# LayerNorm of the convolution branch moved from the compression and prompt stages into the decode passes, and three more right-half projection steps in decode pass 3

## The chip, the cores and the metric

The kernel runs on one core of a Trainium2 chip. The time is the device time of one execution in microseconds, and the number compared is the median over executions. The engines are called by the profile's names: PE is TensorE (matmuls and transposes), PEld its weight loads, DVE is VectorE, ACT ScalarE, POOL GpSimd, SP SyncE, which in this kernel only issues DMAs.

## What is computed

The program is one inference step of a decoder with two layers, for a prompt of 512 rows and 8 sequences of 8 new rows, 576 rows in all, all in float32. A layer has two branches side by side, attention (compressed, selected and window keys) and a Conformer convolution, then one output projection, then a gated feed-forward. The part of the reference that the change touches:

```python
def layer_norm(x, g, b):
    mu = jnp.mean(xf, -1, keepdims=True)
    var = jnp.mean(jnp.square(xf - mu), -1, keepdims=True)
    y = (xf - mu) * lax.rsqrt(var + EPS) * g + b

def conformer_conv(u, buf, w, b, ln_g, ln_b):
    xx = jnp.concatenate([buf, u], 1)
    y = dwconv_valid(xx, w) + b                      # width 31, 512 channels
    y = jax.nn.silu(layer_norm(y, ln_g, ln_b))

def merge_and_ffn(...):
    c, conv_state = conformer_conv(...)
    x = x + jnp.concatenate([o_nsa, c], -1) @ w_out
```

`c` is needed only by the product with `w_out`, which reads it as the last four of eight blocks of 128 channels.

## The kernel before

Channels lie on partitions. `catT` holds the input of the output projection as 8 tiles of 128 channels by 576 rows: tiles 0 to 3 are attention, tiles 4 to 7 (`catT[:, CT + c]`, CT = 4) the convolution. 576 rows are handled as a left and a right half of 288 (HN); `halves()` views a row of 576 as 2x288.

Every engine has its own written-out program, and the order in it is the order in which it works. They meet at named semaphores: `wait_ge(*count("x"))` waits for the next signal of `x`. On DVE, `step(...)` makes an instruction be waited for by the next one. A layer runs through glu, project, compress, prompt, decode, mix, expand and contract.

- **compress** makes compressed keys and values. `hidden` (one of its products: 16 steps j, of 254 columns) accumulates in a PSUM bank that must have been read by DVE's `gelu_in` of an earlier job, which signals `cmp_in`. `keys_T`, `keys_second`, `cmp_scores` and `prompt_values` are short products behind it, each after a small piece of DVE and ACT work. The LayerNorm of the convolution stands here too: `means` (8 matmuls of a matrix of ones with the 4 convolution tiles) sums over channels, DVE's `ln_centre` subtracts the mean in `catT`, ACT squares (`ln_square`), 8 more matmuls (`square_sum`) sum the squares, and DVE's `ln_var` reads them.
- **prompt** is the prompt attention in 16 steps v. DVE's `mask(v)` reads the scores of `scores(v)`, ACT takes the exponentials, DVE's `weight(v)` scales, PE's `turn(v)` transposes and `weigh(v)` applies the values. ACT takes the root of the variance between steps 0 and 1; DVE's reciprocals (`ln_root`) stand behind `weight(1)` and `weight(4)`, and `ln_scale(c)` behind v = 5, 8, 9, 12.
- **decode** has four passes p, two sequences in each. PE makes scores over 2048 keys, then work that DVE's selection (30x30 comparisons, then masks) hides: in passes 0 to 2 steps of `hidden`, in pass 3 steps of the output projection. It then waits for `s_exped` (ACT's exponential of the masked scores), transposes 23 blocks, and weighs the values. Between the last products stand `keys_T`, which wait for DVE's `key_norm` (`kn_made`), and at the end the transpose of the output, which waits for DVE's `o_ready`. A pass also gates one convolution tile (tanh on ACT, two operations on DVE, `conv_done`).
- **mix** finishes the output projection. A unit n is one tile of 128 output channels, 8 steps k of 288 columns for each half. Left halves of units 0 to 3 and eight convolution steps (k = 4 to 7) of right halves (`right_conv`) are done in pass 3, the others here.

SP works through one list as well: keys of the next pass go out when `slc_made` comes, the weights of `w_out` and `w_up` when units are done. `hist`, the convolution history of the next layer (128x4x304), is loaded into the tail of `XC` while layer 0 compresses.

## Time and profile before

| | us |
|---|---|
| median of 3 runs | 1894.15 |
| lowest and highest | 1892.86, 1899.56 |
| profiled execution | 1898.77 |
| its span | 1897.0 |

The span is what the trace covers, and the profiled execution took 1.8 us more than it. Layer 0 fills about the first half of the span, layer 1 the second. In layer 0 compress ends near 220 us, prompt near 308, the four decode passes begin at 308, 345, 382 and 421, and mix at 452. Layer 1 goes through the same places some 935 to 942 us later.

A reader needs three views: the first part of the page (busy time of each engine), the timeline, which merges equal instructions and shows before each the time that its engine sat idle and what ended it, and the windows, which give the busy time of the engines and the granted TensorE clock (1.00 is full) in chosen stretches. In the timeline a float32 matmul counts as two records, so x16 there is 8 matmuls of the program.

### The profile page before, as it was taken

What the parts mean: (1) busy time and instruction counts of PE and PEld (TensorE: products, weight loads), DVE (VectorE), ACT (ScalarE), POOL (GpSimd) and SP (SyncE); (2) the same over time, 40 slices, a digit from 0 to 9 for tenths busy, and PEclk for the clock granted to TensorE, in tenths of its full rate; (3) what the DMA queues carried; (4) which work ended last, traced back from release to release, by engine and by line L of the source; (5) the groups of instructions that cost most, each with busy time, mean ns of one, the idle gap of its engine ahead of it and who ended that gap; (6) DMA issues with size and microseconds to landing.
All of it is one profiled execution on the core that took longest, in us unless ns stands there. A gap on an engine that the chain in (4) does not pass through costs nothing.

```text
span 1897.0 us, 26865 instructions
## 1 busy us (share of the span) xinstructions
PE 1855.6 (98%) x10198; PEld 1414.7 (75%) x10198; DVE 1253.0 (66%) x2636; ACT 371.6 (20%) x957; POOL 118.4 (6%) x219
## 2 busy tenths in 40 slices
PE   8999999999999999999999999998999999999999
PEld 7767677777777777777777676776777777777777
DVE  5899896453666766673268998944536667676631
ACT  2013474322100000100001125832221000000000
POOL 1011400010000000000000113000000000000000
PEclk9999999999999999999999999999999999999999
DMA  7303563673121212131241044057531121222211
GB/s 282 127 1 89 157 204 127 205 241 109 63 67 67 89 67 89 58 133 62 85 161 59 1 141 121 2 179 233 168 109 56 67 89 67 89 67 87 93 61 50
DMA packets 110851, 200.28 MB, mean 106 GB/s; under 512 B 13793, under 2 KB 81650, under 8 KB 105730
## 3 DMA queue, kind: packets, MB, share of 16 engines
q1 hardware_dynamic: 105154, 168.17, 26.6%
q0 software_dynamic: 5568, 30.39, 4.6%
q8 instruction: 81, 1.33, 0.3%
q14 instruction: 48, 0.39, 0.1%
HBM read 190.82 MB, written 15.94 MB: 109 GB/s over the span
## 4 chain that ended last, share of the span: by engine, by line
PE 71%; DVE 20%; SPq 5%; issue 2%; ACT 1%; DMA 1%; POOL 0%; DVEq 0%
PE ps L1048 30%; PE ps L1113 15%; DVE catT L1598 7%; PE ps L612 7%; PE ps L599 5%; PE ps L748 4%; SPq L363 2%; PE ps L851 2%; PE ps L814 2%; PE ps L833 2%; SPq L345 1%; PE ps L899 1%; DVE catT L1605 1%; PE ps L984 1%; DVE rC L1604 1%
## 5 line engine op out<-in xcount | busy, mean ns | idle before, releaser
L1598 DVE SCALAR_TENSOR_TENSOR catT<-XC,par,catT 128x512 f32<-128x512 f32 x240 | 180.3, 751 | 7.5
L2097 DVE TENSOR_TENSOR xT<-xT,ps 128x288 f32<-128x288 f32 (+3 forms) x55 | 41.7, 758 | 153.2 <-PE ps L1113 152.9
L1048 PE MATMUL ps<-catT,rD 128*128 128x288 f32 x528 | 131.6, 406 | 0.0
L1048 PEld LDWEIGHTS ps<-catT,rD 128*128 128x128 f32 x528 | 100.3, 190 | 27.7
L1048 PE MATMUL ps<-catT,XC 128*128 128x288 f32 x480 | 119.8, 406 | 0.4 <-DVE rD L2011 0.4
L748 PE MATMUL ps<-WR,rD 128*128 128x254 f32 (+1 forms) x512 | 119.2, 382 | 0.2
L1463 ACT ACTIVATE rD<-rD 128x592 f32<-128x592 f32 x44 | 30.7, 697 | 450.2 <-DVE rD L2039 450.2
L1048 PE MATMUL ps<-rA,WR 128*128 128x288 f32 x448 | 117.8, 406 | 0.0
L1048 PEld LDWEIGHTS ps<-catT,XC 128*128 128x128 f32 x480 | 91.0, 190 | 26.2 <-issue 1.2
L748 PEld LDWEIGHTS ps<-WR,rD 128*128 128x128 f32 x512 | 93.3, 187 | 18.7 <-issue 2.9
L1048 PEld LDWEIGHTS ps<-rA,WR 128*128 128x128 f32 x448 | 85.1, 190 | 23.5
L612 PE MATMUL ps<-catT,WR 128*128 128x288 f32 x384 | 98.8, 410 | 1.9 <-ACT catT L1212 1.1
L599 PE MATMUL ps<-rA,WR 128*128 128x288 f32 x384 | 93.4, 406 | 0.0
L1048 PE MATMUL ps<-rA,rB 128*128 128x288 f32 x336 | 88.6, 407 | 2.8 <-DVEq L2034 2.8
L748 PE MATMUL ps<-rD 128*128 128x254 f32 x384 | 88.8, 379 | 0.0
L599 PEld LDWEIGHTS ps<-rA,WR 128*128 128x128 f32 x384 | 73.0, 190 | 20.2
L612 PEld LDWEIGHTS ps<-catT,WR 128*128 128x128 f32 x384 | 71.2, 190 | 21.8 <-issue 2.0
L1212 ACT ACTIVATE rC<-ps 128x326 f32<-128x326 f32 (+8 forms) x136 | 48.6, 393 | 191.7 <-PE ps L647 118.9
L1048 PEld LDWEIGHTS ps<-rA,rB 128*128 128x128 f32 x336 | 63.7, 190 | 21.1 <-DVEq L2034 3.7
L748 PEld LDWEIGHTS ps<-rD 128*128 128x128 f32 x384 | 69.7, 188 | 10.3 <-issue 0.7
L647 PE MATMUL ps<-rB,rA 128*128 128x326 f32 x256 | 71.6, 437 | 0.0
L2003 DVE TENSOR_TENSOR rD<-rD,ps 128x288 f32<-128x288 f32 x42 | 19.1, 454 | 77.7 <-PE ps L1048 77.7
(371 smaller groups left out, 3341.8 us busy)
## 6 DMA issues: line engine op xcount, KB each, us to landing
WR<-in_w_up SPq DMA_DIRECT2D x56, 512.0 KB, 3.8
WR<-in_kvc SPq DMA_DIRECT2D x128, 128.0 KB, 2.4
rB<-in_ksT SPq DMA_DIRECT2D x256, 64.0 KB
rB<-in_w_up SPq DMA_DIRECT2D x32, 512.0 KB, 4.4
rD<-in_kvc SPq DMA_DIRECT2D x96, 128.0 KB
rD<-in_w_down SPq DMA_DIRECT2D x8, 1408.0 KB, 7.7
rB<-in_w_down SPq DMA_DIRECT2D x6, 1408.0 KB, 6.2
WR<-in_w_glu SPq DMA_DIRECT2D x16, 512.0 KB, 3.7
```

Of the source, the lines that this page charges most:

```text
L363: sp.dma_start(ksT[e][:, P * g:P * (g + 1)], I["ksT"][l, ds(page, 1)].rearrange("a p e -> (a p) e")).then_inc(sh["ks_in"], 16)
L599: ins = mm(ps[:, bank + hf, 0:HN], w[:, k * P:(k + 1) * P], rhs[:, k, hf * HN:(hf + 1) * HN], start=k == 0, stop=k == K - 1)
L612: ins = mm(ps[:, bank, 0:HN], w[:, k, :], rhs[:, k, hf * HN:(hf + 1) * HN], start=k == first, stop=k == last)
L647: ins = mm(ps[0:m, 4 * (t % 2) + ch, 0:CHW], hT[:, k, t * P:t * P + m], weights(ch, k), start=k == 0, stop=k == KD - 1)
L748: ins = mm(out[:, 0:2 * nb].rearrange("p (c h) -> p c h", h=2), w1[n][:, j, :], chunks[:, j // NPAIR:j // NPAIR + nb, o:o + 2], start=j == ...
L814: ins = mm(ps[:, 2 * e + h, 0:n], q[h], KT[hp[h], e, 0:n], start=True, stop=True)
L833: ins = tr(ps[:, bank, j * P:(j + 1) * P], pb[2 * h + e][:, k * P:(k + 1) * P], ident[:, :])
L1048: ins = mm(ps[:, bank, 0:HN], w[:, k, :], h[:, k, :], start=k == 0, stop=k == 3)
L1113: ins = mm(ps[:, bank, 0:HN], w(k), h(k), start=k == 0, stop=k == FH - 1)
L1212: return act.activation(out, in_, ACT.Copy)
L1598: ins = stt(yc[:, 0:SEQ], xc[:, k:k + SEQ], w, yc[:, 0:SEQ], ALU.mult, ALU.add)
L2097: step(tt(x, x, src, ALU.add))
```

## The change

LayerNorm loses its sums over four tiles. DVE first adds the four convolution tiles into one (`ln_add`, behind `weight(4)`), and PE sums that one over channels with 2 matmuls (`conv_sum`) before `weigh(15)`. DVE subtracts the mean (`ln_centre`) behind the last `weight`. In decode pass 0 DVE squares and adds the tiles itself (`ln_squares`, 7 operations), PE runs `conv_sum` a second time ahead of the value products, and DVE reads it behind the first `key_norm` (`ln_var`). ACT takes the root in pass 1, DVE the reciprocal and two `ln_scale` there, two more in pass 2, then three gates (`conv_gate`) behind pass 2's first `key_norm`; the fourth stays in pass 3. On PE the sums leave compress, and 10 of the 16 steps of a `hidden` that stood in prompt take the place of `means`, now in bank 7; the other 6 stay in prompt. In pass 3, `right_conv` covers 11 steps and not 8: three more stand ahead of the wait for `s_exped`; `mix` has 3 fewer. The buffers of LayerNorm move into the tail of `XC`, so the load of `hist` moves behind pass 3. ACT's four `Square` and its root between prompt steps go away.

```diff
@@ SP, layer
                 sp.wait_ge(*count("uc_out", 16))
-                if l + 1 < DEPTH:
-                    sp.dma_start(XC[:, :, XS0:XW], I["hist"][l + 1]...)
...
+                sp.wait_ge(sh["conv_done"], CT * (l + 1))
+                if l + 1 < DEPTH:
+                    sp.dma_start(XC[:, :, XS0:XW], I["hist"][l + 1]...)
                 down(l, 0)
@@ PE, compress
                 keys_second(l, 1, NCP, prompt_pick, CG[0])
-                means(l)
+                hidden(l, 2, 3, 1, js=range(10))
                 keys_T(NCP)
...
                 prompt_values()
-                for c in range(CT):
-                    square_sum(c, 2, lnsq, CT)
                 keys_T(NCS)
+            def conv_sum():
+                pe.wait_ge(*count("u_ready"))
+                for hf in range(2):
+                    ins = mm(ps[:, 1 + 2 * hf, 0:HN], ones[:, :], lnu[:, hf, :], start=True, stop=True)
+                ins.then_inc(sh["u_summed"], 1)
@@ PE, prompt
                 pe.wait_ge(*count("cs_max"))
-                pe.wait_ge(sh["var_made"], 6 * l + 4)
                 scores(0)
+                hidden(l, 2, 3, 1, js=range(10, 13))
+                scores(1)
+                hidden(l, 2, 3, 1, js=range(13, 16))
                 pe.wait_ge(sh["cmp_in"], 16 * l + 5)
-                hidden(l, 2, 3, 1, js=range(8), bank=4)
-                scores(1)
-                hidden(l, 2, 3, 1, js=range(8, 16), bank=4)
...
+                pe.wait_ge(*count("masked"))
+                conv_sum()
                 weigh(15)
@@ PE, decode
+                    if p == 0:
+                        pe.wait_ge(*count("u_read", 2))
...
                         right_conv(0, 4, CT, KD)
+                        pe.wait_ge(sh["x_left"], KD * l + 2)
+                        right_conv(1, 7, CT, KD - 1)
                     pe.wait_ge(*count("s_exped"))
...
                         pe.wait_ge(*count("st_kept", 2))
+                        if p == 0:
+                            conv_sum()
                     else:
-                        right_conv(1, 6, CT, CT + 2)
+                        right_conv(1, 7, KD - 1, KD)
+                        pe.wait_ge(sh["x_left"], KD * l + 4)
+                        right_conv(2, 5, CT, CT + 1)
...
-                        right_conv(1, 6, CT + 2, KD)
+                        right_conv(2, 5, CT + 1, KD - 1)
@@ ACT
-                root(lnrs[0])
-                root(lnrs[1])
...
+                    if p == 1:
+                        root(lnv)
...
+                        if p == 2:
+                            act.wait_ge(*count("ln_made", 4))
+                            for c in range(3):
+                                act.activation((halves(thl), lnu, lnv)[c], halves(catT[:, CT + c, :]), ACT.Tanh, scale=0.5)...
@@ DVE
+            def ln_squares():
+                y = [halves(catT[:, CT + c, :]) for c in range(CT)]
+                tt(lnu, y[0], y[0], ALU.mult)
+                step(tt(lnv, y[1], y[1], ALU.mult))
+                for c in range(2, CT):
+                    step(tt(lnu, lnu, lnv, ALU.add))
+                    step(tt(lnv, y[c], y[c], ALU.mult))
+                tt(lnu, lnu, lnv, ALU.add).then_inc(sh["u_ready"], 1)
+            def conv_gate(c, th):
+                y = halves(catT[:, CT + c, :])
+                dve.wait_ge(*count("ln_tanh"))
+                step(ts(th, th, 0.5, 0.5, ALU.mult, ALU.add))
+                tt(y, y, th, ALU.mult).then_inc(sh["conv_done"], 1)
@@ DVE, prompt
-                    if v in (1, 4):
-                        ln_root(v // 4)
+                    if v == 4:
+                        ln_add(l)
...
-                    if v in (5, 8, 9, 12):
-                        ln_scale((5, 8, 9, 12).index(v))
+                ln_centre()
@@ DVE, decode
                         gelu_out(*halves_of[1])
+                        if p == 0:
+                            ln_squares()
+                        if p == 1:
+                            ln_root()
                         key_means(NCS)
...
                         key_norm(NCS)
+                        if p == 0:
+                            ln_var()
+                        if p == 1:
+                            ln_scale(0)
+                            ln_scale(1)
+                        if p == 2:
+                            for c in range(3):
+                                conv_gate(c, (halves(thl), lnu, lnv)[c])
                         key_means(NCS)
```

Three places of the order show what moves. The first is PE at the end of compress. L691 is `keys_second`, L735 `keys_T`, L722 `cmp_scores`, L713 `prompt_values`, L664 `means`, L577 `square_sum`, L814 `scores`, L748 `hidden`; before:

```order
L691 MATMUL ps<-par,rC 31x64 x2
L664 MATMUL ps<-catT,ones 128x288 x8
L735 MATMUL ps<-ident,KN 128x31
L691 MATMUL ps<-par,rC 127x64 x2
L722 MATMUL ps<-rC 128x64 x16
L691 MATMUL ps<-par,rC 127x64 x2
L713 MATMUL ps<-par,rC 31x64 x8
L577 MATMUL ps<-rA,ones 128x288 x8
L735 MATMUL ps<-ident,KN 128x127
L814 MATMUL ps<-rC 128x256 x4
L748 MATMUL ps<-WR,rD 128x254 x8
```

and after, where the same functions are L682, L726, L713, L704, L809 and L739:

```order
L682 MATMUL ps<-par,rC 31x64 x2
L739 MATMUL ps<-WR,rD 128x254 x10
L726 MATMUL ps<-ident,KN 128x31
L682 MATMUL ps<-par,rC 127x64 x2
L713 MATMUL ps<-rC 128x64 x16
L682 MATMUL ps<-par,rC 127x64 x2
L704 MATMUL ps<-par,rC 31x64 x8
L726 MATMUL ps<-ident,KN 128x127
L809 MATMUL ps<-rC 128x256 x4
L739 MATMUL ps<-WR,rD 128x254 x3
```

Both groups of eight matmuls with `ones` are gone, ten steps of `hidden` stand where the first group stood, and nothing stands where the second did.

The second place is pass 0 of decode, PE between the last small product and the weighing of the values (L984, after: L985). Before:

```order
L691 MATMUL ps<-par,rC 127x64 [waits cmp_g,vct_kept,st_kept]
L691 MATMUL ps<-par,rC 127x64
L984 MATMUL ps<-rC,rB 32x64 [waits vs_in,st_kept]
L984 MATMUL ps<-rC,rB 32x64 x23
L748 MATMUL ps<-WR,rD 128x254 [waits cmp_in]
L984 MATMUL ps<-rC,rB 32x64 x24
```

and after:

```order
L682 MATMUL ps<-par,rC 127x64 [waits cmp_g,vct_kept,st_kept]
L682 MATMUL ps<-par,rC 127x64
L789 MATMUL ps<-XC,ones 128x288 [waits u_ready,st_kept]
L789 MATMUL ps<-XC,ones 128x288
L985 MATMUL ps<-rC,rB 32x64 [waits vs_in]
L985 MATMUL ps<-rC,rB 32x64 x23
```

The two matmuls with `ones` stand ahead of all value products, and they wait for DVE's `u_ready`. What DVE does there, from `gelu_out` (L1721, after: L1745) to `key_means` (L1725, after: L1749), before:

```order
L1716 SCALAR_TENSOR_TENSOR rC<-rC 128x254 [waits dve_step]
L1721 SCALAR_TENSOR_TENSOR rC<-rC 128x254 [waits cmp_th]
L1725 TENSOR_REDUCE KM<-KN 127x2 [waits kn_sq]
L1726 TENSOR_SCALAR KM<-KM 127x2 [waits dve_step]
L1913 TENSOR_SCALAR st<-st 128x2 [waits s_exped]
```

and after:

```order
L1740 SCALAR_TENSOR_TENSOR rC<-rC 128x254 [waits dve_step]
L1745 SCALAR_TENSOR_TENSOR rC<-rC 128x254 [waits cmp_th]
L1708 TENSOR_TENSOR XC<-catT 128x2x288
L1709 TENSOR_TENSOR XC<-catT 128x2x288
L1711 TENSOR_TENSOR XC<-XC 128x2x288 [waits dve_step]
L1712 TENSOR_TENSOR XC<-catT 128x2x288 [waits dve_step]
L1711 TENSOR_TENSOR XC<-XC 128x2x288 [waits dve_step]
L1712 TENSOR_TENSOR XC<-catT 128x2x288 [waits dve_step]
L1713 TENSOR_TENSOR XC<-XC 128x2x288 [waits dve_step]
L1749 TENSOR_REDUCE KM<-KN 127x2 [waits kn_sq]
L1750 TENSOR_SCALAR KM<-KM 127x2 [waits dve_step]
```

Seven operations on 128x576 elements now stand between the two, and `u_ready` comes with the last of them.

The third place is PE in pass 3, around the wait for `s_exped` ahead of the 16 transposes (L885, after: L880). Before:

```order
L612 MATMUL ps<-catT,WR 128x288 x21
L885 MATMUL ps<-ident,rA 128x128 x16
L885 MATMUL ps<-ident,rA 8x128 x2
L885 MATMUL ps<-ident,rA 127x128
L612 MATMUL ps<-catT,WR 128x288 x2
L984 MATMUL ps<-rC,rB 32x64 x48
```

and after:

```order
L611 MATMUL ps<-catT,WR 128x288 x24
L880 MATMUL ps<-ident,rA 128x128 x16
L880 MATMUL ps<-ident,rA 8x128 x2
L880 MATMUL ps<-ident,rA 127x128
L611 MATMUL ps<-catT,WR 128x288 x2
L985 MATMUL ps<-rC,rB 32x64 x48
```

The run of projection steps ahead of the transposes is longer by three, and what stands behind them is as long as before.

## Rows read from the trace of the kernel before

**Rows 1.** The page, its first part: busy time and instructions of each engine
```profile
PE 1855.6 (98%) x10198; PEld 1414.7 (75%) x10198; DVE 1253.0 (66%) x2636; ACT 371.6 (20%) x957; POOL 118.4 (6%) x219
```

**Rows 2.** Timeline: start us, duration us, engine, line, operation, xcount [idle before <-releaser]
```profile
464.34 15.68 PE L599 MATMUL ps<-catT,WR 128*128 128x288 f32 x64
```

**Rows 3.** Timeline of PE, end of the compression of layer 0 and the first turn
```profile
205.29 4.15 PE L664 MATMUL ps<-catT,ones 128*128 128x288 f32 x16
...
209.71 0.24 PE L735 MATMUL ps<-ident,KN 31*128 31x31 f32 x1 [0.27 <-DVE KN L1732]
...
210.95 3.74 PE L722 MATMUL ps<-rC 128*128 128x64 f32 x32
...
215.48 4.39 PE L577 MATMUL ps<-rA,ones 128*128 128x288 f32 x16
...
220.88 1.13 PE L814 MATMUL ps<-rC 64*128 64x256 f32 x8 [0.90 <-DVE rB L1698]
...
233.57 0.66 PE L833 MATMUL ps<-ident,rA 128*128 128x128 f32 x4 [0.65 <-DVE rC L1716]
```

**Rows 4.** Timeline of DVE in the same stretch
```profile
207.40 0.49 DVE L1716 SCALAR_TENSOR_TENSOR rC<-rC 128x318 f32<-128x318 f32 x1
...
214.73 1.29 DVE L1738 TENSOR_TENSOR rA<-ps,cmpm 128x512 f32<-128x512 f32 x2 [1.21 <-PE ps L722]
...
218.77 0.29 DVE L1732 TENSOR_TENSOR KN<-KN,par 127x128 f32<-127x128 f32 x1
...
227.79 0.69 DVE L1795 CUSTOM_DVE_ANT_0 rC<-ps,causal 128x512 f32<-128x512 f32 x1 [0.84 <-PE ps L814]
```

**Rows 5.** Timeline, PE then DVE, the prompt attention of layer 0
```profile
242.03 1.13 PE L814 MATMUL ps<-rC 64*128 64x256 f32 x8 [0.92 <-DVE st L1798]
...
255.46 1.56 PE L814 MATMUL ps<-rC 64*128 64x384 f32 x8 [0.59 <-DVE st L1798]
...
305.89 1.53 PE L851 MATMUL ps<-rA,rC 128*64 128x128 f32 x24 [0.31 <-ACT rA L1212]
...
210.35 2.76 DVE L1692 TENSOR_TENSOR catT<-catT,rA 128x576 f32<-128x576 f32 x4
...
252.29 1.95 DVE L1702 RECIPROCAL rB<-rB 128x288 f32<-128x288 f32 x1
```

**Rows 6.** Timeline, DVE then PE, decode pass 0 of layer 0
```profile
333.26 0.42 DVE L1721 SCALAR_TENSOR_TENSOR rC<-rC 128x254 f32<-128x254 f32 x1 [0.83 <-ACT rC L1286]
...
336.95 0.88 PE L984 MATMUL ps<-rC,rB 128*32 128x64 f32 x48
```

**Rows 7.** Timeline, DVE then PE, decode pass 1 and the key wait, both layers
```profile
372.96 0.29 DVE L1725 TENSOR_REDUCE KM<-KN 127x2 f32<-127x128 f32 x1 [2.61 <-ACT KN L1290]
...
376.82 0.27 PE L735 MATMUL ps<-ident,KN 127*128 127x127 f32 x1
...
382.28 3.65 PE L899 MATMUL ps<-rB,QB 128*64 128x512 f32 x16 [0.69 <-DMA rB<-in_ksT]
...
1321.94 6.33 PE L899 MATMUL ps<-rB,QB 128*64 128x512 f32 x16 [5.03 <-DMA rB<-in_ksT]
```

**Rows 8.** Timeline, DVE then PE, decode pass 2 of layer 0
```profile
390.21 0.46 DVE L1865 TENSOR_SCALAR rA<-rA 128x576 f32<-128x576 f32 x1 [0.61 <-ACT rA L1400]
...
415.44 0.29 DVE L1732 TENSOR_TENSOR KN<-KN,par 127x128 f32<-127x128 f32 x1
...
418.14 0.28 DVE L1725 TENSOR_REDUCE KM<-KN 127x2 f32<-127x128 f32 x1 [2.40 <-ACT KN L1290]
...
419.76 0.29 DVE L1732 TENSOR_TENSOR KN<-KN,par 127x128 f32<-127x128 f32 x1
...
420.23 0.28 PE L735 MATMUL ps<-ident,KN 127*128 127x127 f32 x1
```

**Rows 9.** Timeline of PE, decode pass 3 of layer 0
```profile
444.20 2.30 PE L885 MATMUL ps<-ident,rA 128*128 128x128 f32 x19 [1.32 <-ACT rA L1408]
```

**Rows 10.** Windows: stretch, length, busy PE PEld DVE ACT POOL, PEclk, DMA, GB/s
```profile
1300.00:1350.00 50.00, 44.13 (x386) 33.03 (x385) 24.67 (x73) 12.56 (x29) 3.37 (x4) 0.93 0.60 190
```

More of the change, by code:

```diff
@@ L205, in build @@
         o += 2 * NT
-        lnsq = [rA[:, 576 * i:576 * (i + 1)] for i in range(2)]
-        lnmu = rA[:, 1152:1728]
-        lnrs = [rA[:, 4192:4192 + HN], rB[:, 5120:5120 + HN]]
+        lnu, lnv = [XC[:, 2 * i:2 * i + 2, XS0:XS0 + HN] for i in range(2)]
         cmp_at = ((rC, o, 2 * NCM), (rC, 5504, 2 * NCS), (rA, 3072, 2 * NCS))
@@ L657, in project @@
                                 ins.then_inc(sh["z_made"], 1)
-            def means(l):
-                pe.wait_ge(sh["tr_kept"], 10 * l + 10)
-                for c in range(CT):
-                    pe.wait_ge(*count("conv_made"))
-                    for hf in range(2):
-                        ins = mm(ps[:, 2 + hf, 0:HN], ones[:, :], catT[:, CT + c, hf * HN:(hf + 1) * HN], start=c == 0, stop=c == CT - 1)
-                ins.then_inc(sh["mu_made"], 1)
             def heads_T(l, t):
@@ L959, in decode @@
                     if not more:
-                        pe.wait_ge(sh["x_left"], KD * l + 2)
-                    turn(range(20, 23), 5 if more else 7).then_inc(sh["st_made"], 1)
+                        pe.wait_ge(sh["x_left"], KD * l + 3)
+                    turn(range(20, 23), 5 if more else 6).then_inc(sh["st_made"], 1)
                     if more:
@@ L1022, in mix @@
                 pe.wait_ge(*count("x_left", 4))
-                for n, bank in enumerate((4, 6, 5)):
-                    half_unit(WR[:, n], bank, 1, rhs=catT, K=KD if n == 2 else CT, first=0 if n == 2 else CT,
-                              last=KD - 1 if n == 2 else CT - 1).then_inc(sh["unit_made"], 1)
+                for n, bank in enumerate((4, 7, 5)):
+                    if n == 2:
+                        half_unit(WR[:, 2], 5, 1, rhs=catT, k0=KD - 1, first=CT, last=CT - 1)
+                    half_unit(WR[:, n], bank, 1, rhs=catT, K=CT, first=CT, last=CT - 1).then_inc(sh["unit_made"], 1)
                 pe.wait_ge(*count("x_upd"))
@@ L1686, in heads, with ln_add, ln_summed @@
                 ins.then_inc(sh["qk_done"], 1)
+            def ln_add(l):
+                dve.wait_ge(sh["uc_out"], 16 * (l + 1))
+                y = [halves(catT[:, CT + c, :]) for c in range(CT)]
+                tt(lnu, y[0], y[1], ALU.add)
+                step(tt(lnv, y[2], y[3], ALU.add))
+                tt(lnu, lnu, lnv, ALU.add).then_inc(sh["u_ready"], 1)
+            def ln_summed(bias):
+                dve.wait_ge(*count("u_summed"))
+                for hf in range(2):
+                    ts(lnv[:, hf], ps[:, 1 + 2 * hf, 0:HN], 1.0 / CC, bias, ALU.mult, ALU.add).then_inc(sh["u_read"], 1)
+                dve.wait_ge(*count("u_read", 2))
@@ L1700, in ln_root @@
-            def ln_root(hf):
+                    y = halves(catT[:, CT + c, :])
+                    ins = tt(y, y, lnv, ALU.subtract)
+                step(ins)
+            def ln_squares():
+                y = [halves(catT[:, CT + c, :]) for c in range(CT)]
+                tt(lnu, y[0], y[0], ALU.mult)
[3 more added lines that the diff above has]
+                    step(tt(lnv, y[c], y[c], ALU.mult))
+                tt(lnu, lnu, lnv, ALU.add).then_inc(sh["u_ready"], 1)
@@ L1817, in prompt @@
                 weight(0)
-                gelu_in(1, NCS, 0, 4)
+                gelu_in(1, NCS, 0)
                 if l:
@@ L1939, in mix @@
                     if n < 4:
[L1940 removed]
+                        add_half(n, (4, 7, 5, 1)[n], 1)
                     else:
```

65 lines of the change are left out of this document (25 added, 40 removed).

## The prediction

> **What bounds the kernel now.** I read the busy times first, then PE's timeline through one layer, then DVE's timeline wherever PE's shows an idle time. PE is busy for 98% of the span [rows 1], so the first guess is that PE work taken away is time taken away. The timeline says where that holds. A run of 64 records of 288 columns takes 15.68 us [rows 2], 0.242 us each with 0.17 us of tail taken off, so 0.485 us for a matmul of the program; by its columns a record of 254 takes 0.214 us. In such runs (projections, feed-forward) PE is the bound. At the end of compress and at the start of prompt it is not: PE waits 0.90 us and 0.65 us for DVE [rows 3], and DVE waits 1.21 and 0.84 us for PE [rows 4], so the two hand one chain to and fro, and what PE does beside it is cover. In decode PE's fill ends 1.32 us before ACT delivers the exponentials in pass 3 [rows 9]. I go through these places in order, for layer 0; layer 1 has the same instructions, so the sum is doubled. All is against the profiled execution (span 1897.0, time 1898.77 us), and carried to the median as a difference.
>
> **End of compress, start of prompt: 12 of 16 matmuls of sums go away in a layer** (the other 4 are the two `conv_sum`). By PE's price that is 12 x 0.485 = 5.8 us, 11.6 us for both layers. I follow the chain instead. Ten steps of `hidden` now stand where `means` began at 205.29 [rows 3], but their bank 7 is free only when `gelu_in` has ended at 207.40 + 0.49 = 207.89 [rows 4]. Twenty records at 0.214 take 4.3 us, so `keys_T` comes at 212.3 and not at 209.71 [rows 3]: 2.6 us late. `cmp_scores` moves from 210.95 [rows 3] to 213.5, and DVE, which waited for it until 214.73 [rows 4], starts at 217.3. Its maximum and key norm took until 218.77 + 0.29 = 219.06 [rows 4], so now 221.6. The squares' sums (4.39 us from 215.48 [rows 3]) and the 0.90 us behind them are gone, so the first `scores` come at 221.8 and not 220.88 [rows 3]: 0.9 us late. DVE's next mask is 0.9 us later too, and here the 0.84 us that DVE idled at 227.79 [rows 4] takes it up, since the next scores are there in time with three steps of `hidden` between and not eight. From that row on DVE's chain stands where it stood, and the first turn at 233.57 waits for DVE's `gelu_in` as before [rows 3]. So the whole PE gain is lost here: **0 us**, bounds -0.9 (the late start fully made up and the 0.65 us wait shortened) and +0.9.
>
> PE then idles for about 3.6 us in one piece, from the end of `prompt_values` near 218.1 to 221.7. The longest idle time at which the rows show PE going on at its full price is the 1.32 us of pass 3 [rows 9]; after 5.03 us the same 16 records took 6.33 us and not 3.65 [rows 7], and that stretch has a granted clock of 0.93 [rows 10], so part of it ran at 1.2 GHz and not at 2.4. The Trainium skill says of this ("TensorE: Matmul & The Clock Gate", section "What's actually happening") that "the default state is throttled, and activity releases the throttle"; by that rule the new idle piece can cost what the row at 1321.94 shows, and it is a rival below.
>
> **Prompt.** DVE loses two reciprocals of 1.95 us [rows 5] and four scalings. The first made PE wait 0.92 us at 242.03 [rows 5], and that wait goes, since the mask then ends 1.95 us earlier: -0.92. The second stands behind `weight(4)`, where `ln_add` now puts three additions of 576 columns; four such operations take 2.76 us [rows 5], about 0.69 each, so 2.1 to 2.2 us for 1.95: the 0.59 us wait at 255.46 [rows 5] grows to 0.8, +0.2. The scalings made nobody wait. `conv_sum` before `weigh(15)` is 4 records, 1.0 us, less most of the 0.31 us wait that follows at 305.89 [rows 5], and I take +0.5 (without that cover +1.0). Its result is read while PE weighs, 2 us before decode needs the banks. Stage: **-0.2 us**, bounds -0.6 and +0.5.
>
> **Decode pass 0.** DVE's `ln_squares` can start behind `gelu_out` at 333.26 + 0.34 [rows 6]. Seven operations on 576 columns, of which five wait for the one before: 0.69 for one that is not waited for (that row of rows 5), and 0.79 for the six others, since the last of a run of four ends 0.07 later than its share and the next starts some 0.03 after that: 5.4 us, so `u_ready` at 339.0. PE's `conv_sum` stands ahead of the value products that began at 336.95 [rows 6]. So PE waits 2.1 us for DVE and then sums for 1.0 us: **+3.1 us**. Nothing takes it up: DVE's `key_means` and `key_norm` follow 2.6 us later, and PE needs them 3.1 us later. Queued behind the wait on PE are all value products, the output and the next pass; SP's fetches of that stretch hang on PE's signals and move along. Bounds +2.0 (DVE ready earlier, sum partly hidden) and +3.6.
>
> **Decode pass 1.** ACT's root, with its table loads, falls where ACT idles. DVE's reciprocal has 576 columns, twice 1.95 = 3.9 us [rows 5], in the 2.61 us that DVE idled until 372.96 [rows 7] and past it by 1.2 us. From a `key_means` to the end of its key norm it is 1.9 us (418.14 to 419.76 + 0.29 [rows 8]), so the key norm was made near 374.9 and `keys_T` stands at 376.82 [rows 7]: of the 1.9 us between, 1.2 are used. The two scalings delay the second `key_means` and the output by 0.2 us. Pass 2 starts with a wait for keys from DMA, 0.69 us in layer 0 and 5.03 us in layer 1 [rows 7], which takes up the 0.2. **0 us**, bounds 0 and +0.6.
>
> **Decode pass 2.** Three gates stand between the first key norm, started at 415.44, and the second `key_means`, at 418.14 after an idle time of 2.40 us [rows 8]. A gate is a scaling of 0.46 us, as at 390.21 [rows 8], and a product of 0.69 [rows 5], about 1.2 us with the wait between; three from 415.65 on let `key_means` in at 419.2. So it, the second key norm and `o_ready` come 1.1 us later. The key norm ended at 420.05 and PE's `keys_T` stood at 420.23 [rows 8], 0.2 us behind: **+1.1 us**, bounds +0.7 and +1.5.
>
> **Pass 3 and mix.** Three steps, 6 records, 1.45 us, move from mix, where PE runs without a gap, to the 1.32 us of idle time before 444.20 [rows 9]. The left half they wait for is added before PE gets there. **-1.3 to -1.45 us**, taken as -1.4; zero if that addition were late. The load of `hist` (0.62 MB) goes, in layer 0, ahead of `w_down` and the second half of `w_out`. PE needs the first of those weights at 464.34 [rows 2] less 1.45 us, 11 us behind pass 3. At the 190 GB/s that rows 10 show over a stretch in which DMA was asked for only in part, the load takes 3.3 us. I take 0 us, with +1 as the upper end for layer 0.
>
> **Sum.** Per layer 0 - 0.2 + 3.1 + 0 + 1.1 - 1.4 = +2.6, so +5.1 us for both with the roundings: 1898.77 becomes 1903.9 in an execution like the profiled one, and the median 1894.15 becomes 1899.3.
>
> **Rivals.** (a) *PE's removed work reaches the end.* For it: 98% busy. Against it: the chain above, step by step. It would give 1899.3 - 11.6 = 1887.7. (b) *The key wait of layer 1 gets short.* It is 5.03 us and 2.7 us of slow matmuls against 0.69 us in layer 0 [rows 7]; runs differ by 6.7 us, and this wait may be why. If the longer pass 0 lets the transfers ahead of those keys drain, up to 4.3 + 2.7 = 7.0 us go, and the median becomes 1892.3 if it held the whole wait. Against it: SP's list behind pass 0 hangs on PE's signals as before. (c) *The clock falls in the new 3.6 us of idle time*, the slower side: the place is the wait for the key norm ahead of the first `scores`; the point from which it decides lies between 1.32 us, which left the price alone, and 5.03 us, which did not; the price by the row of that wait is 6.33 - 3.65 = 2.7 us per layer, on the chain, since scores feed the masks. That gives 1899.3 + 5.4 = 1904.7. (d) *The three steps do not fit*: if they wait for the added left half, the 1.4 us are not won, 1902.1.
>
> **How the numbers follow.** Forecast 0.52, (a) 0.10, (b) 0.14, (c) 0.14, (d) 0.05, and 0.05 for a gain beyond (a), such as a shorter chain at the start of prompt together with (b). About 0.5% is what a measurement of this kernel can tell from no change, 9.5 us here: faster than 1884.7 has 0.06 (from the last case and the edge of (a)), slower than 1903.6 has 0.14 (from (c), and from (d) with the upper bounds), same has 0.80. The forecast's own bounds are 1895 to 1903. The range reaches down over most of (b) and to (a)'s edge, and up to (c): 1889 to 1904.5.
>
> **What would show it.** In the trace after: a wait of PE for DVE's `gelu_in` before the ten steps (2.6 us) and one of 3.6 us before the last `keys_T`, with the first turn no earlier after `merged` than before; the 0.92 us wait gone; PE waiting 2.1 us for `XC` of DVE in pass 0 and some 1.1 us for the key norm in pass 2; no wait of 1.3 us in pass 3; mix 1.45 us shorter. I am wrong if the first turn comes several us earlier, if pass 0 shows no wait for DVE, or if the granted clock drops at the start of prompt.

## The result, and the profile after

The changed kernel takes 1908.85 us (median of 6 runs, 1906.58 to 1911.64) beside 1893.86 us for the kernel before on the same chip: a ratio of 1.0068, interval 1.0051 to 1.0085. The time rose by 15.0 us where 5.1 were forecast, and lies above the range of 1889 to 1904.5. The profiled execution took 1907.97 us (span 1906.2), 9.2 us more than the profiled one of before.

The page after, its first part, answers [rows 1]:

```profile
PE 1855.1 (97%) x10150; PEld 1415.4 (74%) x10150; DVE 1266.6 (66%) x2648; ACT 366.4 (19%) x947; POOL 118.5 (6%) x219
```

PE has 48 records fewer (24 matmuls of 288 columns, 11.6 us by [rows 2]) and is busy for 0.5 us less. So what is left has become dearer. The timeline of PE at the end of compress (start us, us, engine, line, what, idle time in brackets) shows where; L739 is `hidden`, L726 `keys_T`, L713 `cmp_scores`, L809 `scores`, L828 the first turn; it answers [rows 3]:

```profile
207.71 6.26 PE L739 MATMUL ps<-WR,rD 128*128 128x254 f32 x20 [2.58 <-DVE rC L1740]
...
215.15 3.74 PE L713 MATMUL ps<-rC 128*128 128x64 f32 x32
...
223.31 0.47 PE L726 MATMUL ps<-ident,KN 127*128 127x127 f32 x1 [3.56 <-DVE KN L1756]
223.71 2.08 PE L809 MATMUL ps<-rC 64*128 64x256 f32 x8
225.72 2.91 PE L739 MATMUL ps<-WR,rD 128*128 128x254 f32 x6
...
233.54 0.71 PE L809 MATMUL ps<-rC 64*128 64x128 f32 x8 [0.62 <-DVE st L1820]
236.47 2.01 PE L828 MATMUL ps<-ident,rA 128*128 128x128 f32 x8 [2.22 <-DVE rC L1740]
```

The two forecast waits stand there, 2.58 us (2.6) and 3.56 us (3.6). But 20 records of `hidden` take 6.26 us and not 4.3, and the `scores` that took 1.13 us in [rows 3] take 2.08. The wait of 2.22 us for `gelu_in` ahead of the first turn was 0.65 us in [rows 3] and was not forecast. Layer 1 has the first wait too, but there the same 20 records take 4.60 us:

```profile
1151.82 4.60 PE L739 MATMUL ps<-WR,rD 128*128 128x254 f32 x20 [2.58 <-DVE rC L1740]
```

DVE in the stretch of layer 0, which answers [rows 4], now waits longer for `cmp_scores` (1.21 us in [rows 4]). It also waits for the first `scores`, which it found ready before; the 0.84 us of [rows 4], for the second `scores`, are gone:

```profile
218.92 1.29 DVE L1762 TENSOR_TENSOR rA<-ps,cmpm 128x512 f32<-128x512 f32 x2 [2.78 <-PE ps L713]
225.84 0.43 DVE L1817 CUSTOM_DVE_ANT_0 rA<-ps,causal 128x256 f32<-128x256 f32 x1 [1.27 <-PE ps L809]
```

Windows of the changed kernel (stretch, length, busy PE PEld DVE ACT POOL, PEclk, DMA share, GB/s) say why:

```profile
208.00:212.00 4.00, 4.00 (x12) 3.19 (x12) 1.07 (x4) 0.15 (x1) 0.69 (x1) 0.57 0.35 94
222.00:229.00 7.00, 5.69 (x17) 3.51 (x19) 5.52 (x18) 2.79 (x8) 4.84 (x9) 0.53 0.48 119
235.50:242.00 6.50, 5.46 (x22) 3.20 (x24) 5.41 (x27) 4.54 (x16) 1.61 (x4) 0.50 1.19 397
345.00:348.00 3.00, 3.00 (x78) 2.19 (x69) 0.76 (x3) 0.00 (x0) 0.00 (x0) 0.50 0.69 204
1287.00:1290.00 3.00, 3.00 (x78) 2.19 (x74) 1.02 (x3) 0.00 (x0) 0.00 (x0) 0.50 0.68 214
```

The granted clock is at or near 0.50 in them, 1.2 GHz and not 2.4. Layer 1 has two more such stretches, at 1164 and 1181. Each stands behind or across one of the new waits. The kernel before has the full clock in those places in the execution that was profiled first and in a second one (the "before_look1" of the experiments), whose windows these are:

```profile
206.00:214.00 8.00, 7.24 (x47) 6.00 (x45) 7.18 (x17) 2.49 (x7) 0.88 (x2) 1.00 0.37 101
222.00:229.00 7.00, 6.92 (x32) 4.60 (x30) 5.97 (x18) 4.99 (x12) 3.13 (x7) 1.00 0.40 132
235.00:242.00 7.00, 5.75 (x50) 3.84 (x48) 6.79 (x24) 4.74 (x15) 1.55 (x3) 1.00 1.08 350
343.00:348.00 5.00, 4.92 (x41) 2.27 (x40) 3.10 (x9) 1.29 (x5) 2.18 (x3) 1.00 0.79 257
```

A third execution of it ("before_look2") lost the clock once behind the first turn, with waits of 0.63, 0.31 and 0.54 us ahead. So the kernel before is not wholly free of such stretches; the changed kernel has seven of them between the end of compress and the end of pass 0, four in layer 0 and three in layer 1, at the same places in both of its profiled executions. The window of that third execution:

```profile
235.00:242.00 7.00, 6.46 (x44) 4.28 (x44) 6.76 (x24) 3.50 (x12) 1.62 (x3) 0.76 1.04 354
```

Pass 0 has the forecast wait of 2.1 us. DVE's timeline (the last of its seven operations) and then PE's answer [rows 6]. Groups of 48 records of the value products took 0.88 us and take 1.32 and 1.46 us:

```profile
342.35 0.76 DVE L1713 TENSOR_TENSOR XC<-XC 128x576 f32<-128x576 f32 x1
```

```profile
343.25 1.21 PE L789 MATMUL ps<-XC,ones 128*128 128x288 f32 x4 [2.11 <-DVE XC L1713]
344.39 1.32 PE L985 MATMUL ps<-rC,rB 128*32 128x64 f32 x48
...
346.78 1.46 PE L985 MATMUL ps<-rC,rB 128*32 128x64 f32 x48
```

The key wait of layer 1, 5.03 us in [rows 7], is 1.04 us in the changed kernel. In pass 2 PE waits 0.80 us for the second key norm, where three gates on DVE end at 427.23 + 0.76, which answers [rows 8]. In pass 3 the wait of [rows 9] is gone, and `mix` has 42 records where it had 48. DVE's timeline, then PE's:

```profile
427.23 0.76 DVE L1732 TENSOR_TENSOR catT<-catT,XC 128x576 f32<-128x576 f32 x1
```

```profile
429.87 0.33 PE L726 MATMUL ps<-ident,KN 127*128 127x127 f32 x1 [0.80 <-DVE KN L1756]
...
453.96 2.30 PE L880 MATMUL ps<-ident,rA 128*128 128x128 f32 x19
...
462.59 10.45 PE L611 MATMUL ps<-catT,WR 128*128 128x288 f32 x42 [0.53 <-ACT catT L1217]
...
1333.91 3.65 PE L896 MATMUL ps<-rB,QB 128*64 128x512 f32 x16 [1.04 <-DMA rB<-in_ksT]
```

To see the stages apart I cut each profiled execution at the same rows: the four records of `keys_second` ahead of the old `means` (the 31-key form), the first turn, the start of the keys' product of each pass, and the end. Each cell is layer 0 / layer 1 in us; the first row is the time at which layer 0's cut begins. That row differs for a reason outside the change: 11 of the 14 profiled executions, of whatever kernel, have a stretch at 1.2 GHz between 12 and 23 us, and the one of 202.99 has none. So I compare from the first cut on. "Unread matmuls" (matmuls whose results nobody reads) and "few sums" are kernels of the experiments below, put here so that one table serves; "combined" has three of the change's pieces placed otherwise.

| stage | before | changed | changed, unread matmuls | before, few sums | combined, unread matmuls |
|---|---|---|---|---|---|
| up to the first cut | 204.95 | 204.71 | 202.99 | 206.16 | 204.77 |
| end of compress to first turn | 28.62 / 28.68 | 31.76 / 30.05 | 29.02 / 28.92 | 35.27 / 35.36 | 26.37 / 26.39 |
| first turn to pass 0 | 74.63 / 74.55 | 75.86 / 75.71 | 74.17 / 74.12 | 74.56 / 74.56 | 74.18 / 74.17 |
| pass 0 | 36.67 / 36.65 | 41.52 / 41.52 | 39.91 / 39.92 | 36.67 / 36.67 | 37.63 / 37.63 |
| pass 1, with pass 2's key wait | 37.41 / 41.76 | 36.68 / 37.80 | 37.18 / 37.55 | 37.35 / 37.33 | 36.71 / 36.74 |
| pass 2 | 38.89 / 41.57 | 40.40 / 39.89 | 39.89 / 40.33 | 38.90 / 38.89 | 38.89 / 38.88 |
| pass 3 and the rest | 719.13 / 533.49 | 717.90 / 532.40 | 717.66 / 533.04 | 719.16 / 533.52 | 717.71 / 532.03 |
| span | 1897.0 | 1906.2 | 1894.7 | 1904.4 | 1882.1 |

### The profile page after: what moved, and what is told of

It reads as the page before. It is cut to its first block, busy times and chain, and to the rows that moved or that the text cites. A ratio compares the mean times of both kernels' runs of the same rounds, so it can differ in the third digit from the quotient of the medians.

```text
span 1906.2 us, 26767 instructions
## 1 busy us (share of the span) xinstructions
PE 1855.1 (97%) x10150; PEld 1415.4 (74%) x10150; DVE 1266.6 (66%) x2648; ACT 366.4 (19%) x947; POOL 118.5 (6%) x219
## 4 chain that ended last, share of the span: by engine, by line
PE 71%; DVE 21%; SPq 3%; issue 2%; ACT 1%; DMA 1%; POOL 0%; DVEq 0%
PE ps L1053 30%; PE ps L1118 15%; PE ps L611 8%; DVE catT L1596 7%; PE ps L598 5%; PE ps L739 4%; PE ps L809 2%; PE ps L846 2%; PE ps L828 2%; SPq L361 2%; SPq L343 1%; PE ps L896 1%; DVE catT L1603 1%; PE ps L985 1%; DVE rC L1602 1%
## 5 line engine op out<-in xcount | busy, mean ns | idle before, releaser
L739 PE MATMUL ps<-WR,rD 128*128 128x254 f32 (+1 forms) x512 | 125.0, 394 | 5.2 <-DVE rC L1740 5.2
L739 PEld LDWEIGHTS ps<-WR,rD 128*128 128x128 f32 x512 | 96.5, 194 | 25.5 <-DVE rC L1740 5.5
L739 PE MATMUL ps<-rD 128*128 128x254 f32 x384 | 88.9, 379 | 0.3 <-DMA rD<-in_kvc 0.3
L739 PEld LDWEIGHTS ps<-rD 128*128 128x128 f32 x384 | 69.9, 188 | 10.8 <-issue 0.7
```

The source lines that it names most:

```text
L739: ins = mm(out[:, 0:2 * nb].rearrange("p (c h) -> p c h", h=2), w1[n][:, j, :], chunks[:, j // NPAIR:j // NPAIR + nb, o:o + 2], start=j == ...
```

## The experiments

**Theory C**: the waits are as forecast, and what the sum lacks is the clock, which falls to 1.2 GHz around the new idle places. **Rival W**: the waits and what they push back cost more than summed, and the clock costs nothing. I tried C from both sides: keep PE busy in the changed kernel, and take PE's work away in the kernel before.

**Unread matmuls in the changed kernel.** In four places, or in the three of compress and prompt alone:

```diff
+            def filler(n, bank):
+                for _ in range(n):
+                    mm(ps[:, bank, 0:HN], ones[:, :], xT[:, 0, 0:HN], start=True, stop=True)
...
+                filler(5, 2)
                 hidden(l, 2, 3, 1, js=range(10))
...
                 prompt_values()
+                filler(7, 2)
                 keys_T(NCS)
...
                 scores(2)
+                filler(4, 6)
...
                         if p == 0:
+                            filler(4, 1)
                             conv_sum()
```

> The changed kernel with extra matmuls (ones by the first half of x, 288 columns, the sums are read by nobody) in the four new idle places of PE in each layer: 5 before the ten steps of hidden, 7 before the last keys_T, 4 behind scores(2), 4 before conv_sum of decode pass 0. Nothing of the computation is left out. They take about the time of the waits (2.4, 3.4, 1.9 and 1.9 us at 0.485 us each). Theory C (the missing term is the clock that falls to 1.2 GHz around these waits): granted clock 1.00 from 200 us to the end of pass 0, no stretch at 0.5 there, and the time falls by about 10 to 14 us against the changed kernel, to 1895 to 1899. Theory W (the waits themselves cost more than I summed, the clock costs nothing): the time stays at 1909 or rises by up to 3 us, since the extra matmuls can only stand in the way.

> As the run with all extra matmuls, without the four in decode pass 0. Theory C: the start of prompt is where most of the loss is (8.5 us of span at 1.2 GHz in layer 0, 1.7 us of it in pass 0), so it has nearly the whole gain: 1897 to 1901, and the stretch at 0.5 in pass 0 of layer 0 (near 344) stays. If pass 0 is the larger part, it is at 1904 or more.

All four: 1900.69 us, ratio to before 1.0031 (1.0012 to 1.0050). The three: 1901.95 us, 1.0030 (1.0010 to 1.0049). So 40 more matmuls made the changed kernel 8.2 us faster (32 of them 6.9 us), still 1.7 us above the range that I gave for the one and 1.0 us for the other. The two kernels were not timed side by side; by their ratios to the kernel before, 1.0068 and 1.0031, the gain is 7 us. The three places at the start have most of it. PE's timeline and the windows of the kernel with all four:

```profile
203.33 2.69 PE L767 MATMUL ps<-xT,ones 128*128 128x288 f32 x10
205.98 4.60 PE L739 MATMUL ps<-WR,rD 128*128 128x254 f32 x20
...
216.28 3.66 PE L767 MATMUL ps<-xT,ones 128*128 128x288 f32 x14
219.92 0.33 PE L726 MATMUL ps<-ident,KN 127*128 127x127 f32 x1
220.18 1.13 PE L815 MATMUL ps<-rC 64*128 64x256 f32 x8
```

```profile
206.00:210.00 4.00, 4.00 (x20) 3.47 (x20) 1.32 (x5) 0.43 (x1) 0.69 (x1) 1.00 0.31 86
220.00:227.00 7.00, 6.72 (x35) 4.15 (x36) 6.58 (x20) 2.78 (x10) 4.72 (x10) 1.00 0.33 74
230.00:237.00 7.00, 6.06 (x44) 3.71 (x42) 6.75 (x33) 5.52 (x18) 3.96 (x8) 1.00 0.98 296
```

PE does the unread work in the time of the waits (2.69 us for 2.58, 3.66 for 3.56), the granted clock is 1.00, the 20 records take 4.60 us and not 6.26, and the scores 1.13 and not 2.08. W falls. From the first cut on the execution is 1691.7 us long against 1701.5 for the changed kernel, and I put these 9.8 us down to the clock: 10.4 us by the table lie between the first cut and the end of pass 0, where the slow stretches are, and the other stages give back 0.6 us. It is the fastest of this kernel's 12 executions; the medians differ by 8.2 us, and the granted clock of the others is 0.994 to 1.000, so most of them still lost something.

The kernel with three had something that I had not expected. Its 2.11 us wait in pass 0 stayed, and the clock did not fall there: pass 0 took 39.98 us in layer 0, as with the fourth filled. The row of that wait, and the window behind it:

```profile
337.11 1.21 PE L795 MATMUL ps<-XC,ones 128*128 128x288 f32 x4 [2.11 <-DVE XC L1720]
```

```profile
338.00:348.00 10.00, 9.93 (x217) 6.49 (x217) 4.67 (x15) 1.84 (x7) 2.82 (x4) 1.00 0.49 129
```

So the same wait had a stretch at 1.2 GHz behind it in one kernel and none in the other, as the 2.58 us wait had in layer 0 of the changed kernel and not in layer 1. What decides it stays open.

**PE's sums taken out of the kernel before**, all else unchanged. In each layer 6 of the 8 matmuls of `means` are left out, and 6 of the 8 of `square_sum` have 2 columns and not 288, so LayerNorm's mean and variance are not the right ones and only the time counts. It takes nearly as much of the sums from PE as the change does, without any of its moves:

```diff
-                    for hf in range(2):
+                    for hf in range(2 if c == CT - 1 else 0):
-                        ins = mm(ps[:, 2 + hf, 0:HN], ones[:, :], catT[:, CT + c, hf * HN:(hf + 1) * HN], start=c == 0, stop=c == CT - 1)
+                        ins = mm(ps[:, 2 + hf, 0:HN], ones[:, :], catT[:, CT + c, hf * HN:(hf + 1) * HN], start=True, stop=True)
...
-                    square_sum(c, 2, lnsq, CT)
+                    pe.wait_ge(*count("sq_made"))
+                    w = HN if c == CT - 1 else 2
+                    for hf in range(2):
+                        ins = mm(ps[:, 2 + hf, 0:w], ones[:, :], lnsq[c % 2][:, hf * HN:hf * HN + w], start=True, stop=True)
+                    ins.then_inc(sh["sq_summed"], 1)
```

> The kernel before with 12 of the 16 matmuls of LayerNorm's sums left out in each layer (means sums only the last tile, of each tile of squares but the last two columns are summed), all else as it was; so LayerNorm's mean and variance are those of one tile. Rival (a) of the prediction (PE is the bound there): 12 x 0.485 us per layer go, the time falls by 11.6 us, to 1884. The chain theory: only the two waits of DVE for PE (1.21 and 0.84 us) can be taken out, so at most 2 us per layer, 4 us in all: 1892; with theory C the new idle places of PE can bring stretches at 1.2 GHz and take this back: 1892 to 1898.

1908.29 us, ratio 1.0066 (1.0043 to 1.0089): taking matmuls away made it 15 us slower. Both theories missed the size (I had said 1892 to 1898), and rival (a) of the prediction missed the sign.

PE's timeline, DVE's, and the windows of this kernel:

```profile
207.75 1.21 PE L664 MATMUL ps<-catT,ones 128*128 128x288 f32 x4 [1.17 <-DVE catT L1610]
210.93 0.31 PE L735 MATMUL ps<-ident,KN 31*128 31x31 f32 x1 [1.97 <-DVE KN L1736]
...
212.63 7.04 PE L722 MATMUL ps<-rC 128*128 128x64 f32 x32
```

```profile
219.70 1.29 DVE L1742 TENSOR_TENSOR rA<-ps,cmpm 128x512 f32<-128x512 f32 x2 [4.96 <-PE ps L722]
```

```profile
210.50:230.50 20.00, 17.97 (x85) 15.45 (x86) 11.42 (x25) 5.83 (x14) 11.06 (x18) 0.50 0.59 174
1152.50:1172.50 20.00, 18.07 (x85) 15.54 (x86) 11.45 (x26) 5.83 (x14) 13.41 (x23) 0.50 0.49 142
```

Waits of 1.17 and 1.97 us with little between them stand ahead of 20 us at 0.50. `cmp_scores` takes 7.04 us and not 3.74 [rows 3], and DVE waits 4.96 us for it. The whole loss is in the first stage of the table: +6.65 and +6.68 us. The other stages are those of before within 0.1 us, except passes 1 and 2 of layer 1, where the profiled execution of before holds its key wait. So the sums that the change takes from PE had covered waits, and with that had kept its clock at this place.

**The later `conv_sum` of pass 0**, ahead of `keys_T` and not of the value products:

```diff
                         pe.wait_ge(*count("st_kept", 2))
-                        if p == 0:
-                            conv_sum()
...
                                 first_left(3, 4)
+                            if p == 0:
+                                conv_sum()
                             keys_T(NCS)
```

> The changed kernel with the conv_sum of decode pass 0 moved from ahead of the value products to just ahead of pass 0's keys_T, so that DVE's squares have the value products as cover. Nothing is left out. By my sum the wait of 2.1 us goes in each layer and the 1.0 us of sums stays: -4.2 us, and with the stretch at 1.2 GHz that stands beside this wait (1.7 us in layer 0) up to -7.5: 1901.5 to 1904.7. If the wait only moves (DVE's key norm or the softmax chain is the bound there), 1908 to 1909.

1901.20 us, ratio 1.0013 (0.9993 to 1.0034): 7.65 us under the changed kernel, 0.3 us beyond the far end of what was expected with the clock. The wait is gone and pass 0 takes 37.63 us (351.91 less 314.28) in place of 41.52. That is 3.9 us per layer, of which the wait was 2.1 us:

```profile
314.28 3.65 PE L896 MATMUL ps<-rB,QB 128*64 128x512 f32 x16 [0.38 <-ACT catT L1217]
...
346.23 1.13 PE L789 MATMUL ps<-XC,ones 128*128 128x288 f32 x4
347.20 0.27 PE L726 MATMUL ps<-ident,KN 127*128 127x127 f32 x1
...
351.91 3.65 PE L896 MATMUL ps<-rB,QB 128*64 128x512 f32 x16
```

**The ten steps of `hidden` split**, four ahead of the first `keys_T` and six ahead of the last, alone:

```diff
-                hidden(l, 2, 3, 1, js=range(10))
+                hidden(l, 2, 3, 1, js=range(4))
                 keys_T(NCP)
...
                 prompt_values()
+                hidden(l, 2, 3, 1, js=range(4, 10))
                 keys_T(NCS)
```

> Only the split of the ten steps (four ahead of the first keys_T of the main part, six ahead of the last) on the changed kernel. Nothing is left out. Waits alone: the 3.6 us idle piece ahead of the first scores falls to about 1 us and the first turn comes 1.3 us earlier per layer: 1906. Theory C: the stretch at 1.2 GHz ahead of and in the first scores (3.4 us lost by its granted clock in each layer) goes as well, since the engine is no longer idle there; the one before it (behind the 2.6 us wait for gelu_in) and the one at the first turn may stay: 1899 to 1903.

1905.67 us, ratio 1.0053 (1.0034 to 1.0072). That is the 1906 of the waits alone, not the 1899 to 1903 of C, so here C's forecast missed. The profiled execution (1908.88 us) is above its median. The wait before the last `keys_T` fell to 0.77 us and in layer 0 the `scores` there took 1.14 us again, but layer 1 lost the clock from 1149.0 to 1166.5, in half-microsecond windows: from the first cut to the first turn it took 27.78 us in layer 0 and 33.15 us in layer 1, with the same instructions: the clock that C expected to win back came back in one layer, and the other lost more than in the changed kernel (30.05 us there). In layer 0 the clock still fell behind the 2.58 us wait and at the first turn. Its runs spread from 1900 to 1910. What makes the one layer keep its clock and not the other stays open.

**The three steps of `right_conv`**, alone on the kernel before, and taken back from the changed kernel:

```diff
                         right_conv(0, 4, CT, KD)
+                        pe.wait_ge(sh["x_left"], KD * l + 2)
+                        right_conv(1, 7, CT, KD - 1)
```

> The kernel before with one part of the change alone: the three more steps of right_conv in pass 3 (and the banks that this takes); LayerNorm, hidden and the load of hist stay as they were. My sum gives -1.4 us per layer, -2.8 in all: 1891. Rival: the steps do not fit in front of the exponentials or the left half that they wait for comes late: no change, 1894. If the 11 steps keep the clock up or let DMA drain, at most another 1 us.

> The changed kernel with the three extra steps of right_conv put back into mix (and their banks), so that LayerNorm's move stands alone. Nothing is left out. The runs of the changed kernel lie close together, so the three steps are weighed better here than on the kernel before: by my sum 1.4 us per layer come back, 1911.7 (between 1910.5 and 1913). If the three steps bring nothing, 1909; if they are worth what the fastest runs of the run with the three alone suggest (3.4 us), 1912.4.

Alone they give 1894.26 us, ratio 0.9989 (0.9968 to 1.0011), which by itself decides nothing, since the runs of before in that comparison spread from 1889.8 to 1911.3. The fastest run of each (1886.35 and 1889.76) differ by 3.4 us. Its profiled execution lost the clock for 7 us in compress of layer 1, where it has the sums and the waits of before, so that 32 records of `cmp_scores` took 5.13 us and not 3.74:

```profile
1145.11 5.13 PE L722 MATMUL ps<-rC 128*128 128x64 f32 x32
```

Without the three steps the changed kernel takes 1911.29 us, ratio 1.0095 (1.0080 to 1.0111), 2.4 us more than with them, where 2.8 were expected. The traces agree better: the stage "pass 3 and the rest" of layer 0 is 719.13 us in before and 717.65 with the steps added, and 717.90 in the changed kernel and 719.15 with them taken back.

**The changed kernel and the kernel before again.**

> The changed kernel unaltered, so that these runs and the ones before them have it beside them on one chip. If its runs are as narrow as the six so far: 1905 to 1912, granted clock 0.987 to 0.991. If the kernel before owes its fast runs to this chip, its median moves and the ratio comes nearer to 1.005.

> The kernel before, unaltered, one look. Its runs spread from 1889 to 1911. Theory K: the wait of 5.0 us for the keys of layer 1's pass 2 in the profiled execution, with its 3.4 us of lost clock, belongs to that execution and not to the kernel: here the wait is under 1.5 us and the span is 1888 to 1893 with a clock of 0.998 or more. Rival: it is there each time, and the span is 1895 or more.

> As the first look: under theory K a wait for layer 1's keys under 1.5 us, or, if it is longer, a span longer by the wait and its stretch at 1.2 GHz.

The changed kernel: 1909.15 us, ratio 1.0073 (1.0048 to 1.0099). The kernel before took 1892.03 us in the one (span 1890.2), with a key wait of 0.23 us, and 1899.94 us in the other (span 1898.2), with 6.06 us. Their rows, one of each:

```profile
1317.14 3.65 PE L899 MATMUL ps<-rB,QB 128*64 128x512 f32 x16 [0.23 <-DMA rB<-in_ksT]
```

```profile
1323.42 6.02 PE L899 MATMUL ps<-rB,QB 128*64 128x512 f32 x16 [6.06 <-DMA rB<-in_ksT]
```

So theory K holds: the 5.03 us wait of [rows 7] and the slow matmuls behind it belong to some executions of the kernel before and not to others, and the three profiled do not say how often. Why the keys come late in those stays open.

**The moves together.** The split, the later `conv_sum`, and two of pass 2's three gates put behind `o_ready` (with PE's waits for `conv_done`, not shown); then the same with unread matmuls in two places:

```diff
-                            for c in range(3):
-                                conv_gate(c, (halves(thl), lnu, lnv)[c])
+                            conv_gate(0, halves(thl))
...
+                    if p == 2:
+                        conv_gate(1, lnu)
+                        conv_gate(2, lnv)
```

```diff
+                filler(5, 2)
                 hidden(l, 2, 3, 1, js=range(4))
...
                 scores(2)
+                filler(4, 6)
```

> The changed kernel with three moves, nothing left out: the ten steps of hidden are split, four ahead of the first keys_T and six ahead of the last; conv_sum of pass 0 stands ahead of pass 0's keys_T; and in pass 2 only the first gate stands behind the first key norm, the other two behind o_ready. Both theories agree on the waits: the keys of compress come 6 steps x 2 x 0.214 = 2.6 us earlier, which takes that much off the 3.6 us wait and some 1.3 us off the way to the first turn (per layer), pass 0 gives 3.9 us per layer as in the run with the later sum, pass 2 gives 0.8. Without a clock effect: 2 x (1.3 + 3.9 + 0.8) = 12 us under the changed kernel, 1897. Theory C expects more, since with a shorter wait most of the stretches at 1.2 GHz at the start of prompt go too: 1889 to 1892, under the kernel before.

> The combined kernel (hidden split 4 and 6, later conv_sum of pass 0, two of three gates later) with the unused extra matmuls in two of the places where it is still idle: 5 behind the 8 steps of the samples' part (the 2.6 us wait for gelu_in), 4 behind scores(2) (the 1.5 and 2.2 us around the first turn). Nothing is left out. Theory C: its three stretches at 1.2 GHz in each layer's start of prompt go, cmp_scores take 3.74 us again and not 5.18, the first turn comes some 2 us earlier per layer: 1884 to 1889 in an undisturbed execution, a median of 1888 to 1892. Rival: DVE's own chain sets the first turn, so that PE's clock there costs nothing more: the time stays at the combined kernel's 1894 (or rises by what the extra matmuls stand in the way).

Together: 1894.84 us, ratio 1.0005 (0.9987 to 1.0024), 2.8 us above what C gave, below the 1897 without it. Its clock is still 0.987 to 0.995, and `cmp_scores` takes 5.18 us. With the unread matmuls: 1885.53 us, ratio 0.9956 (0.9941 to 0.9970). This one beats both kernels, the only one that does. PE's timeline and the windows:

```profile
205.11 2.69 PE L767 MATMUL ps<-xT,ones 128*128 128x288 f32 x10
207.76 2.00 PE L739 MATMUL ps<-WR,rD 128*128 128x254 f32 x8
...
210.93 3.74 PE L713 MATMUL ps<-rC 128*128 128x64 f32 x32
```

```profile
200.00:250.00 50.00, 45.87 (x339) 33.65 (x337) 41.37 (x133) 24.25 (x76) 19.55 (x33) 1.00 0.72 223
1150.00:1200.00 50.00, 45.71 (x389) 31.95 (x391) 44.63 (x185) 36.34 (x112) 11.28 (x21) 1.00 0.23 65
```

The stage from compress to the first turn is 2.3 us per layer shorter than in before, pass 0 costs 1.0 us more (the two sums) and pass 2 nothing. The rival, that DVE's chain makes the clock there worth nothing, falls: the two kernels differ in 18 unread matmuls alone and by 9.3 us in the medians. The profiled executions differ by 7.4 us from the first cut on; the one of the combined kernel is the fastest of its 12 and had kept the clock in compress of layer 1.

## Why the prediction was wrong, point by point

**The waits that were named were right.** Forecast and found: 2.6 and 2.58 us before the ten steps, 3.6 and 3.56 before the last `keys_T`, 2.1 and 2.11 in pass 0, no wait in pass 3, `mix` 1.46 us shorter. In pass 2 the wait is 0.80 us where 1.1 were named. One place was missed: "the first turn at 233.57 waits for DVE's `gelu_in` as before". Ten of the 16 steps of `hidden` that had filled PE's time between the first `scores` and the first turn now stood ahead of them, so PE waits 0.62 and 2.22 us there and not 0.65. By itself that costs little (with the clock at 1.00 the stage took 29.0 us for 28.6), but it is one of the places where the clock fell.

The stages of the changed kernel with unread matmuls, where the clock is 1.00, test the sum without the clock. Start of prompt: 0 forecast, +0.4 and +0.2 found. Prompt: -0.2, found -0.5 and -0.4. Pass 0: +3.1, found +3.2 and +3.3. Pass 2: +1.1, found +1.0 in layer 0 (in layer 1 the 41.57 of before holds slow matmuls). Pass 3 and mix: -1.4, found -1.5 in layer 0 and -0.45 in layer 1 (combined with unread matmuls: -1.4 and -1.5). From the first cut on it is 6.7 us longer than the kernel before in the execution without the key wait (1691.7 and 1890.2 - 205.15 = 1685.05): the sum was +5.1. Two starts in the working of passes 0 and 2, 333.26 + 0.34 and 415.65, are not the ends of the rows named but some 0.1 us earlier, at the start of the next instruction; the trace after has the same 0.34 us (337.38 to 337.72).

**The step that failed is the clock**, which the sum put at 0 us. I had it among the rivals, (c), with 0.14, at one place (the 3.6 us), at 2.7 us per layer, and had named a drop at the start of prompt as a sign of being wrong. The mechanism of (c) was right and three things about it were wrong. The place: the changed kernel shows it also behind the 2.58 us wait, at the first turn (waits of 0.62 and 2.22 us) and in pass 0, four places in layer 0 and not one. The waits that count: I took the two waits of pass 0 and of `gelu_in` as harmless, though they lie in the same gap between 1.32 and 5.03 us in which I had left the 3.6 us open. The size: 9.8 us in the profiled execution, not 5.4. And I read the removed sums as cover that is lost for the chain alone; they were also what kept PE going, as the kernel with few sums shows (+15 us with no other change). The forecast's +5.1 and these 9.8 make 14.9, beside the 15.0 that the medians moved; that they meet so closely is in part luck, since the traces have 6.7 and 9.8, 16.5 us from the first cut on, and the unread matmuls gave back 8.2 us by the medians. The rule that the prediction cited (the Trainium skill, "TensorE: Matmul & The Clock Gate", section "What's actually happening") agrees in direction with the granted clock of 0.50 in these windows. The sentence quoted does not say at which waits the clock is lost; the traces here show it lost at several, and not each time at the same one.

**Rival (b) was a misreading of the baseline.** The profiled execution of before held the key wait of layer 1. Its median run was not traced, but at 1893.9 us it is nearer to the execution without the wait (1892.0) than to those with it (1898.8 and 1899.9), so (b) counted 7.0 us off a median in which they were most likely already missing. That fits the two profiled executions differing by 9.2 us only and the medians by 15.0: pass 1 and pass 2 of layer 1 give back 5.6 us in the profiled pair.

**Rival (a)** (1887.7) is refuted in place: less PE work without other changes gave more time. **(d)** did not occur: the three steps fit, and the wait for the exponentials is gone.

## What to carry to other kernels

Where PE waits often for another engine, the matmuls that stand between are also what holds its clock: before work is moved off PE, list each new wait with the waits that stand near it, and price the work behind each at 1.2 GHz as a possible loss, not only behind the longest. An unread matmul in such a wait cost next to nothing here where it fitted (pass 0: 39.9 us with it, 40.0 without), and 18 and 40 of them were worth 9 and 8 us in two kernels; it is a quick test of whether the clock is the cause. And look at a second profiled execution before a long wait for DMA is taken into the sum.

## What was not expected of the hardware

Waits of 2.58 us, and of 1.17 and 1.97 us with 1.2 us of matmuls and a little more between, were followed by stretches at 0.50 of 4 to 20 us, in which PE was busy for up to 4.00 of 4.00 us. The same 2.11 us wait in pass 0 was followed by the low clock in the changed kernel and not in the one with unread matmuls some 100 us earlier, and the 2.58 us wait by the low clock in layer 0 and not in layer 1. In one execution of the kernel before with the three steps alone, the clock fell in compress with no wait longer than 0.48 us in the 15 us before. So these traces do not let one name beforehand each place where the clock falls, and the times of one kernel can spread by it: 1900 to 1910 us for the split, at clocks from 0.986 to 0.994. In few sums PE at 1.2 GHz made DVE wait 4.96 us for `cmp_scores`; that such lateness feeds further waits and keeps the clock low is my reading and was not tested apart.
